# Banded attention with values stationary and transposed probabilities moving, and forget rows in the low-part matmul

## What is computed

```python
# first block, forgetting attention ("fox"): 4 heads of 64, causal
cum = jnp.cumsum(jax.nn.log_sigmoid(f_logit + f_bias), axis=1)
sc = q @ k.T * scale + cum_q - cum_k                 # then mask, softmax, @ v
# first block, chunked attention: 4 heads of 64, band of 9 chunks, bias from a table
sc = q @ k.T * scale + bias                          # then mask, softmax, @ v
# second block, banded attention ("swa"): 16 heads of 64, 2 key/value heads,
# per query block of 128: its own 128 keys and the 128 before
s = qn @ kn.T + pos_bias                             # masked to the band
m = max(max(s), sink);  p = exp(s - m)
p = p / (sum(p) + exp(sink - m))
y = ((p @ vn) * silu(z)) @ w_out
```

## Time and profile before

| | |
|---|---|
| median of 3 runs | 2418.8 us (2418.34 to 2423.13) |
| profiled execution, its own time | 2419.9 us, span 2418.1 us |
| PE busy | 2360.1 us, 98% of the span |
| DVE, ACT, POOL busy | 1507.1, 833.2, 1251.0 us |
| chain that ended last | PE 84%, DVE 6%, issue 4%, POOL 3%, ACT 2% |

### The profile page before, as it was taken

How to read it: one execution, slowest core, us unless ns; L and a number is a source line. 1 busy time by engine, 2 the same in 40 slices (tenths; PEclk the granted TensorE clock), 3 DMA queues, 4 the chain that set the end, 5 groups by cost and what they waited for, 6 DMA issues and landing times.

```text
span 2418.1 us, 32914 instructions
## 1 busy us (share of the span) xinstructions
PE 2360.1 (98%) x11836; PEld 1964.2 (81%) x11836; DVE 1507.1 (62%) x1911; ACT 833.2 (34%) x1588; POOL 1251.0 (52%) x712
## 2 busy tenths in 40 slices
PE   7999999999999999999999999999999999999998
PEld 6887788888887888888888878878888788888887
DVE  6725555624567678888877778773754866045565
ACT  4211545612433222222222433131232333055663
POOL 4533864134145666666668444563745634465523
PEclk9999999999999999999999999999999999999999
DMA  6511000031011333333331111111221113100023
GB/s 214 161 44 45 1 1 20 17 113 44 18 41 48 105 122 121 121 121 121 119 122 61 64 35 47 59 61 62 70 77 58 60 64 132 53 27 19 27 103 133
DMA packets 67270, 177.31 MB, mean 73 GB/s; under 512 B 6846, under 2 KB 13760, under 8 KB 65112
## 3 DMA queue, kind: packets, MB, share of 16 engines
q1 hardware_dynamic: 58344, 148.58, 18.6%
q10 hardware_dynamic: 8816, 27.25, 3.3%
HBM read 160.04 MB, written 15.72 MB: 73 GB/s over the span
## 4 chain that ended last, share of the span: by engine, by line
PE 84%; DVE 6%; issue 4%; POOL 3%; ACT 2%; DMA 1%; SPq 0%; DVEq 0%; POOLq 0%; ACTq 0%
PE ps L690 23%; PE ps L693 22%; PE ps L691 22%; PE ps L849 6%; PE ps L827 4%; PE ps L837 3%; POOL split_lo L1605 1%; DVE h_lo L564 1%; PE ps L705 1%; PE ps L704 1%; PE ps L703 1%; PE ps L495 1%; DVE h_lo L567 1%; DVE trail L3220 0%; ACT p L979 0%
## 5 line engine op out<-in xcount | busy, mean ns | idle before, releaser
L690 PE MATMUL ps<-h_hi,split_hi 128*128 128x512 f32 (+1 forms) x1576 | 627.2, 398 | 20.3 <-DVE h_lo L567 13.6
L691 PE MATMUL ps<-h_lo,split_hi 128*128 128x512 f32 (+1 forms) x1576 | 612.8, 389 | 0.0
L693 PE MATMUL ps<-h_hi,split_lo 128*128 128x512 f32 (+1 forms) x1576 | 547.6, 389 | 0.0
L1481 POOL TENSOR_TENSOR split_hi<-raw,cf 128x1024 fp32r<-128x1024 f32 x70 | 137.2, 1961 | 492.4 <-PE ps L693 386.9
L690 PEld LDWEIGHTS ps<-h_hi,split_hi 128*128 128x128 f32 x1576 | 297.9, 189 | 79.6 <-issue 11.4
L693 PEld LDWEIGHTS ps<-h_hi,split_lo 128*128 128x128 f32 x1576 | 297.4, 189 | 61.6
L691 PEld LDWEIGHTS ps<-h_lo,split_hi 128*128 128x128 f32 x1576 | 298.0, 189 | 55.0 <-issue 0.2
L1556 POOL TENSOR_TENSOR split_lo<-raw,split_hi 128x512 fp32r<-128x512 f32 x144 | 231.8, 1629 | 198.2 <-ACT split_hi L2493 196.6
L1605 POOL TENSOR_TENSOR split_lo<-raw,split_hi 128x512 fp32r<-128x512 f32 x84 | 127.6, 1528 | 179.8 <-ACT split_hi L2651 179.8
L1483 POOL TENSOR_TENSOR split_lo<-raw,split_hi 128x1024 fp32r<-128x1024 f32 x70 | 195.9, 2799 | 5.5
L2493 ACT CAST split_hi<-raw 128x512 fp32r<-128x512 f32 x144 | 86.8, 622 | 287.3 <-PE ps L693 214.0
(11 more groups left out here) (442 smaller groups left out, 5126.4 us busy)
## 6 DMA issues: line engine op xcount, KB each, us to landing
raw<-in_strips SPq DMA_DIRECT2D x208, 256.0 KB, 2.8
raw<-in_strips SPq DMA_DIRECT2D x86, 512.0 KB, 3.5
ada_raw<-in_ada SPq DMA_DIRECT2D x64, 512.0 KB, 3.9
memw_raw<-in_mem_strips SPq DMA_DIRECT2D x8, 512.0 KB, 6.0
xT<-in_xT ACTq DMA_DIRECT2D x4, 1024.0 KB, 8.1
x_spill_d<-xT ACTq DMA_DIRECT2D x1, 3584.0 KB, 10.0
xT<-x_spill_d ACTq DMA_DIRECT2D x2, 1792.0 KB, 9.2
out_T<-out_sb SPq DMA_DIRECT2D x14, 256.0 KB, 3.0
```

Source lines behind the costliest of these rows:

```text
L690: pe.matmul(acc[:, a:b], w_hi, hi[:, a:b], start=first, stop=False)
L691: pe.matmul(acc[:, a:b], w_hi, lo[:, a:b], start=False, stop=False)
L693: mm = pe.matmul(acc[:, a:b], w_lo, hi[:, a:b], start=False, stop=last)
L1481: pool.tensor_tensor(hi, raw[:, r, :], ones[:, 0:1].to_broadcast([P, D]), ALU.mult).then_inc(hi_split, 1)
```

## The change

Banded attention gets an order of its own, and no longer goes through `attention_plan`:

- Units run head by head (kv major in a tile). Transposed probabilities of two units (a pair, 3 or 4 blocks of 128) lie side by side in one bank; ACT copies them as the fp32r high part `swa_pt_hi` and DVE takes the low part `swa_pt_lo`.
- Values are stationary: `swa_v[kv]` holds, for each key block, 64 columns of the values' high part and 64 of the low part. For each key block the queries of one or two blocks move, once in the high and once in the low part. The outputs come out feature-major in banks 6 and 7, high-value and low-value products on different halves of the partitions; ACT copies one half (`swa_out_part`), DVE adds the other (`swa_out_sum`).
- The inverse row sums are written by DVE as 64 equal columns for each query block (`swa_inverse`, the last block in `rinv`), transposed by PE (`swa_rows`) and multiplied into `swa_z` by DVE (`swa_inverse_gate`); the outputs are multiplied in by POOL (`swa_gate`), for the last tile by DVE (`last_gate`).
- The maximum is taken as a negated minimum of -s - bias starting from the negated sink, so `floor` goes, here and in chunked attention; the exponential gets scale -1. ACT issues the exponential of unit u + 1 ahead of the copy.
- In forgetting attention the rows of cumulated logs (three fp32r parts, through `cum_d` in DRAM) and of ones lie in the free half of `fox_second` and of the low parts of the keys; the augmented matmul, `fox_aug` and the head mask go. The DMAs that bring them are issued by POOL, and PE waits for `aug_in` ahead of unit 32.
- The output product has 12 pieces inside the stage and 4 behind it; the low part of strip 2 is made by DVE.

```diff
-                dve.tensor_tensor_reduce(unit_probs(a, u), s, unit["bias"], 1.0, -3.0e38,
-                                         ALU.add, ALU.max, rowmax[:, u:u + 1]).then_inc(a["biased"], 1)
-            def floor(u):
-                unit = units[u]
-                if unit["bias"] is not None:
-                    a["n_biased"] += 1
-                    reached(dve, a, "biased", a["n_biased"])
-                    dve.tensor_scalar(negmax[:, u:u + 1], rowmax[:, u:u + 1], -3.0e38 if unit["sink"] is None else unit["sink"],
-                                      -1.0, ALU.max, ALU.mult).then_inc(a["max_ready"], 1)
+                dve.tensor_tensor_reduce(unit_probs(a, u), s, unit["bias"], -1.0, 3.0e38,
+                                         ALU.add, ALU.min, negmax[:, u:u + 1]).then_inc(a["max_ready"], 1)
...
-                       (fox_stack(h, t), fox_klo(h)[:, lo:hi], lo, hi),
-                       (fox_aug[:, h, q_tok], aug_k[:, lo:hi], lo, hi)] for lo, hi in key_banks(n)]
+                       (fox_second[:, h, q_tok], fox_klo(h)[:, lo:hi], lo, hi)] for lo, hi in key_banks(n)]
...
-            sp.wait_ge(cum_parts, 3)
-            sp.wait_ge(aug_in, 32)
-            part = [mraw[0:HEADS, 5, :].bitcast(BF16)[:, 0:T], mraw[0:HEADS, 5, :].bitcast(BF16)[:, T:2 * T],
-                    mraw[0:HEADS, 4, :].bitcast(BF16)[:, 0:T]]
-            for r in range(3):
-                sp.dma_start(aug_q[r:P:32, :], part[r]).then_inc(aug_done, 16)
-                sp.dma_start(aug_k[r + 3:P:32, :], part[r]).then_inc(aug_done, 16)
+            sp.wait_ge(cum_parts, AUG_ROWS)
+            for r, part in enumerate((mraw[0:HEADS, 5, :], mraw[0:HEADS, 4, :], cum_last[0:HEADS, :])):
+                sp.dma_start(cum_d[r], part).then_inc(cum_out, 16)
...
-            pool.wait_ge(aug_done, 16 * 6)
+            for a, b in ((0, AUG_ROWS), (2 * AUG_ROWS, HD)):
+                pool.dma_start(fox_second[HD + a:HD + b, :, :], dram["aug"][0, a:b].bitcast(F32R)).then_inc(aug_in, 16)
+            pool.wait_ge(cum_out, 16 * AUG_ROWS)
+            pool.dma_start(fox_second[HD + AUG_ROWS:HD + 2 * AUG_ROWS, :, :], cum_d.bitcast(F32R)).then_inc(aug_in, 16)
...
+                high(fox_second[0:HD, h, :], fox_q[r, h // 2, :], r)
                 high(fox_khi(h)[r, :], fox_k[r, h // 2, :], r)
                 high(fox_khi(h)[other, :], fox_k[r, h // 2, :], r)
-                low(fox_klo(h)[other, :], fox_k[r, h // 2, :], fox_khi(h)[r, :])
-                low(fox_klo(h)[r, :], fox_k[r, h // 2, :], fox_khi(h)[r, :])
-            for h in range(HEADS):
-                half_split(pool.tensor_tensor(fox_aug[:, h, :], aug_q[:, :],
-                                              cf[:, C_HEAD + h:C_HEAD + h + 1].to_broadcast([P, T]), ALU.mult))
+                low(fox_klo(h)[0:HD, :], fox_k[r, h // 2, :], fox_khi(h)[r, :])
+            for low_pair, a in ((fox_raw, 0), (fox_kr, 2)):
+                pool.dma_start(low_pair[HD:HD + AUG_ROWS, :, :], cum_d[:, a:a + 2, :].bitcast(F32R)).then_inc(aug_in, 16)
+                pool.dma_start(low_pair[HD + AUG_ROWS:P, :, :], dram["aug"][1, AUG_ROWS:HD, 0:2].bitcast(F32R)).then_inc(aug_in, 16)
...
+        SWA_AHEAD = 2
+        SWA_STEPS = range(-SWA_AHEAD, SWA_UNITS + 4)
...
+        PAIR_KEYS = ((0,), (2, 1), (4, 3), (6, 5, 7))
+        KEY_ORDER = [kb for keys in PAIR_KEYS for kb in keys]
...
+        OUT_PIECES = {OUT_FROM: (0, 0), OUT_FROM + 4: (0, 1), OUT_FROM + 5: (1, 0), OUT_FROM + 7: (0, 2), OUT_FROM + 9: (1, 1),
+                      OUT_FROM + 11: (0, 3), OUT_FROM + 13: (0, 4), OUT_FROM + 15: (1, 2), OUT_FROM + 17: (0, 5),
+                      OUT_FROM + 19: (0, 6), OUT_FROM + 21: (1, 3), OUT_FROM + 23: (1, 4)}
...
+            def swa_turn(u):
+                m, probs = u // 2, swa_probs(u)
+                n = swa_unit(u)[3] // P
+                at = 0 if u % 2 == 0 else swa_blocks(m)[1] - 2
+                if u % 2 == 0:
+                    reached(pe, att_swa, "copied_dve", m - 1)
+                    if u - 1 in ROWS_AT and rows_in_pair(ROWS_AT[u - 1][0]):
+                        tile, half = ROWS_AT[u - 1]
+                        reached(pe, att_swa, "o_gate", 2 * tile + half + 1)
+                reached(pe, att_swa, "exp_done", u + 1)
+                for j in range(n):
+                    mm = pe.transpose(swa_turned(m)[:, (at + j) * P:(at + j + 1) * P], probs[:, j * P:(j + 1) * P], ident)
+                mm.then_inc(att_swa["turned"], 1)
+            def swa_weigh(m):
+                h = m // 4
+                reached(pe, att_swa, "copied_dve", m + 1)
+                for kb in PAIR_KEYS[m % 4]:
+                    value = swa_v[h % 2][:, kb, :]
+                    for half, col0, block, n in key_spans(kb):
+                        fresh = kb % 4 == 0
+                        last = kb == NK - 1 or half == 0 and kb == 3
+                        if fresh:
+                            reached(pe, att_swa, "normed", 2 * h - 1 + half)
+                        o, blocks = bank(6 + half, n * P, col0), slice(block * P, (block + n) * P)
+                        pe.matmul(o, value, swa_pt_hi[:, blocks], start=fresh, stop=False)
+                        mm = pe.matmul(o, value, swa_pt_lo[:, blocks], start=False, stop=last)
+                    mm.then_inc(att_swa["weighted"], 1)
+            def swa_rows(tile, half):
+                reached(pe, att_swa, "inverse", sums_needed(tile, half))
+                if rows_in_pair(tile):
+                    reached(pe, att_swa, "copied_dve", (ROWS_STEP[tile, half] - 1) // 2)
+                else:
+                    pe.wait_ge(bin_q, 2 * (tile + 2) + 1)
+                    reached(pe, att_swa, "o_gate", 2 * tile + half)
+                for j in range(4):
+                    mm = pe.transpose(inverse_rows(tile, half)[:, j * P:(j + 1) * P], inverse_columns(4 * half + j), ident)
+                mm.then_inc(att_swa["o_turned"], 1)
...
+            for u in SWA_STEPS:
+                if 0 <= u < SWA_UNITS:
+                    swa_turn(u)
+                if u + SWA_AHEAD < SWA_UNITS:
+                    swa_score(u + SWA_AHEAD)
+                if u in ROWS_AT:
+                    swa_rows(*ROWS_AT[u])
+                swa_beside(u)
+                if u % 2 == 0 and 2 <= u <= SWA_UNITS:
+                    swa_weigh(u // 2 - 1)
+            early_out(0, 7)
+            for k in range(5, NK):
+                early_out(1, k)
+            reached(pe, att_swa, "o_gate", 2 * NK)
...
+            def swa_high(m):
+                h = m // 4
+                reached(act, att_swa, "turned", 2 * m + 2)
+                if h:
+                    reached(act, att_swa, "weighted", QT * (h - 1) + blocks_weighed(m))
+                act.copy(swa_pt(swa_pt_hi, m), swa_turned(m)).then_inc(att_swa["copied_act"], 1)
...
+            def swa_maximum(u):
+                reached(dve, att_swa, "scored", u + 1)
+                reached(dve, att_swa, "turned", u - 3)
+                h, n = u // QT, swa_unit(u)[3]
+                dve.tensor_tensor_reduce(swa_probs(u), swa_scores(u), swa_bias[:, h, 2 * P - n:2 * P], -1.0, neg_sinks[:, h:h + 1],
+                                         ALU.add, ALU.min, negmax[:, u:u + 1]).then_inc(att_swa["max_ready"], 1)
+            def swa_low(m):
+                reached(dve, att_swa, "copied_act", m + 1)
+                dve.tensor_tensor(swa_pt(swa_pt_lo, m), swa_turned(m), rows(swa_pt(swa_pt_hi, m)), ALU.subtract)\
+                   .then_inc(att_swa["copied_dve"], 1)
+            def swa_out_sum(h, half):
+                main, _ = head_rows(h)
+                at = swa_out(h, half)[main, :]
+                reached(dve, att_swa, "o_hi", 2 * h + half + 1)
+                dve.tensor_tensor(at, bank(6 + half)[main, :], at, ALU.add).then_inc(att_swa["normed"], 1)
+            def swa_inverse_gate(tile, half):
+                dve.wait_ge(bin_z, tile + 1)
+                reached(dve, att_swa, "o_turned", 2 * tile + half + 1)
+                at = swa_z_half(tile, half)
+                dve.tensor_tensor(at, inverse_rows(tile, half), at, ALU.mult).then_inc(att_swa["o_gate"], 1)
+            def last_gate(half):
+                tile = NK - 1
+                reached(dve, att_swa, "o_mid", 2 * tile + half)
+                reached(dve, att_swa, "normed", 4 * tile + 3 + half)
+                reached(dve, att_swa, "o_gate", 2 * tile + half + 1)
+                dve.tensor_tensor(swa_z_half(tile, half), swa_out(2 * tile, half), swa_z_half(tile, half), ALU.mult)\
+                   .then_inc(att_swa["o_mid"], 1)
...
+                if u + SWA_AHEAD < SWA_UNITS:
+                    swa_maximum(u + SWA_AHEAD)
+                if u % 2 == 1 and 0 < u < SWA_UNITS:
+                    swa_low(u // 2)
+                if u in ROWS_AT and rows_in_pair(ROWS_AT[u][0]):
+                    swa_inverse_gate(*ROWS_AT[u])
+                if u in SINK_AT:
+                    n, h, u0, u1 = SINK_AT[u]
```

(30 more changed lines are left out.)

315 lines of the change are left out of this document (184 added, 131 removed).

## The result

The changed kernel takes 2436.22 us (median of 4 runs, 2435.95 to 2436.64) against 2420.91 for the kernel before on the same chip: ratio 1.0069, 95% interval 1.0058 to 1.0081. It is slower by 0.7%. The profiled execution took 2436.64 us, its span is 2434.5 us, its mean granted clock 0.993.

What follows compares the result with a forecast made beforehand. PE, busy 98% of the span, was taken as the bound. 2419.9 - 19.2 + 24.6 + 19 + 8 - 8.3 - 1 = 2443 us, or 2442 with the median's 1.1 off; range 2412 to 2462.

Steps and rivals of the forecast that it cites:

- PE's own work: Banded attention: weighing falls from 3.30 to 2.10 us a head, all PE work from 12.81 to 11.61; -19.2 us.
- The block and what waits for it: Banded head start: DVE's 4.15 us of sums and wide reciprocals makes PE wait 2.2 or 1.8 us; +24.6 us.
- the chain: Banded head start: from last score matmul through DVE's queue until PE starts the next weighing, 6.05 us.
- the cover of 3.81 us: Banded head start: PE's work until that weighing: products, one weighing, transposes and scores; 3.81 us.
- the maximum stays: Banded attention, DVE: the maximum keeps its price, 0.34 + 0.10 us with its accumulator read.
- the walk of the last tile: Last banded tile, step by step: PE waits 24 us there and behind it, against 6 before; +19 us.
- the clock's term: Banded attention: granted clock falls after five of about 18 waits, 1.6 us each; +8 us, bounds 0 and 30.
- Forgetting attention: Forgetting stage: the matmuls against augmented rows go, and added POOL DMAs fit their cover; -8.3 us.
- Chunked attention: Chunked stage: 32 floors leave the chain maximum, exponential, transpose; -1 us (0 to -2.7).
- Rival 1: Banded attention: DVE keeps ahead, PE stays the bound; 2397 us, if the block is under about 1.9 us; chance 0.15.
- Rival 2: Banded attention: waits half absorbed, clock stays up; the 24.6 halves, last tile +10; 2410 to 2424 us; chance 0.13.
- The estimate of 8.3 ns a column: DVE reciprocals by the Trainium skill's page: block 1.06 us longer, total some 17 us higher; the trace's 6.25 was preferred.

Runs made afterwards that it cites:

- the fastest kernel: Changed kernel with 8-column reciprocals, broadcast copies on DVE, both small DVE instructions replaced, and output products and DVE's last low part reordered at the drain: 2398.14 us.
- the small reciprocals with the small instructions replaced: Changed kernel with 8-column reciprocals and broadcast copies; sink argument moved to ACT's bias, row-sum addition in the maximum's reducing form: 2404.62 us.
- the two runs with zeros added: Changed kernel plus zero-adding matmuls at four waits in the last tile: 64 of 32 columns, 2437.85 us; 32 of 512 columns, 2435.4 us.
- The small reciprocals: Changed kernel with reciprocals of 8 columns in place, and two copies broadcasting them to the 448 and 64 columns: 2406.56 us.
- the kernel with the doubled block: Changed kernel with the 448-column reciprocal issued twice, output unchanged: 2513.51 us.

## Why the prediction came out as it did

**PE's own work.** Predicted -19.2 us. In the fastest kernel, whose banded instructions on PE are the changed kernel's and whose clock is 1.00 as before, PE is busy 186.9 us of the stage, where it was 204.7: -17.8. Two heads take 23.16 us where waits are nearly gone (the small reciprocals with the small instructions replaced), for the 2 x 11.61 of the prediction. The product of 12 x 0.12 and 6 x 0.11 us a head holds.

**The block and what waits for it.** The 448-column reciprocal measured 2.953 us for 2.95, the 64-column one 0.495 for 0.55, the chain 6.06 for 6.05. The waits were 1.80 us on even heads and 1.08 + 0.37 on odd ones, for 2.2 and 1.8. So two heads came to 27.15 and not 27.3, and up to the first score of the 105th unit (start of the last tile's two-step lead) the stage is 7.8 us longer (173.8 for 166.0), where my terms gave some 9 (24.6 less 13 heads at 1.20). The chain was right, the cover of 3.81 us was a few tenths too short. I did not see one price: "the maximum stays". It takes 478 ns for 424, and 349 for 291 with 128 columns. The chunked maxima, which got the same negated minimum but start from a constant, kept their 824 ns. So the 54 to 58 ns belong to the start value that is read from SBUF, at both widths.

**The last tile and the clock.** Terms of 19 and 8 us, 27 in all. Measured from the 105th unit's score to the end of the stage: 61.3 us for 43.4, +17.9; with the 4 us put back that PE itself saved in those three heads and a bit, 22. The clock fell four times, all of them in this part, and not five times among 18 waits: behind the waits of 1.8 us in the steady part it stayed at 1.00 (window 2109 to 2284 above; in the two runs with zeros added it fell once there). It was low for 20.5 us, where five falls of 3.4 make 17, so that the time at half clock was not the error. What the falls cost was mis-sized: I took 1.6 us each, which the steady part bears out, but in the last tile much of PE's work at half clock lies in time in which it would wait for DVE. By the estimate above 3.4 to 4.8 us stand where I had 8, and 17 to 18.5 where I had 19: the walk of the last tile was near, the clock's term about twice too large.

**Forgetting attention.** Predicted -8.3, measured -6.6 in four kernels alike. The matmuls went (48 fewer), but PE now waits 1.5 us for exponentials there (L843 on ACT), where it waited 0.4: with scores done sooner, ACT's exponential is the next in line, a wait that I had not asked for. The other 0.6 us are not accounted for. The forget rows were never late: POOL's seven more DMAs found their cover.

**Chunked attention.** Predicted -1. From the first chunked score to the first banded one, with all that lies between, it is 1715.0 us for 1715.2. The floors had been hidden; DVE idle on PE's scores there had said so.

**The start.** 2.8 us that I did not forecast and that isn't the change's: 1.2 up to the wait at 232 us, and 1.6 by the missing fall of the clock behind it. The earlier trace rows showed such a fall in one execution; the same wait has it in some executions and not in others. I took it as something that follows from the wait.

**The rivals.** Rival 1 (2397 us, DVE keeps ahead) named its own condition, a block below about 1.9 us. The small reciprocals make one of some 1.7 us (0.16, 0.20, 0.43, 0.18 and an output sum of 0.69), and the time is 2406 and, with DVE's waits for POOL and the drain cleared, 2398. Rival 2 (waits half absorbed) did not hold: the steady waits kept four fifths of their forecast (1.63 us a head on average for 2.05), and the last tile cost 17 to 18.5 us and not 10; only the clock's falls were half absorbed. The estimate of 8.3 ns a column stays refuted: 2953 ns for 448 columns and 203 for 8 are 6.25 ns a column.

**The sum, as measured:** 2419.9 - 2.8 - 6.6 - 0.2 + 25.7 + 0.6 behind the stage and around the span = 2436.6 us for the profiled execution. The banded stage's 25.7 stand against 32.4 (-19.2 + 24.6 + 19 + 8). Against the forecast's 2443 for this execution, most of the difference is the clock's share (about 4 us) and the start (2.8), with forgetting attention (1.7) and chunked attention (0.8) the other way: part of the nearness of the total is errors that cancel.

## What to carry to other kernels

Broadcast after a reciprocal and not before it: here a reciprocal costs 6.25 ns for every column that it writes, a copy under 1 (425 ns for 448). An engine that is idle on average can still set the pace if its new work stands in one piece at the head of a queue; count from the last instruction that feeds it to the first that waits for what is queued behind, and compare with what the other engine has to do until then. When a burst is cut up or moved, look at what POOL does at the new place: small DVE instructions between SBUF operands may wait there until POOL's instruction ends (up to 2.16 us in these runs), and the profile books this as their busy time.

## What the runs showed of the hardware

- DVE instructions with all operands in SBUF (a tensor by a scalar, two tensors, a copy, and the reducing form too) that start during a POOL instruction last until it ends: 8 columns took up to 2.16 us, 4 columns up to 1.78. Reciprocals, and forms with one operand in PSUM, keep their durations.
- A start value read from SBUF makes the add-and-minimum form 54 to 58 ns longer, at 128 and at 256 columns.
- A fall of the granted clock costs 1.6 us where PE is the bound (28.73 for 27.16 us; 95.95, 94.3 and 92.7 us with two, one and none). In the same place and behind the same wait it comes in one execution and not in another: behind 2.08 us at 231 us in the kernel with the doubled block and not in the changed one, which are the same up to there; at the head of the last tile in one of the two runs that differ only in the drain, 1.2 us.
- 64 matmuls of 32 columns in PE's idle time did not keep the clock up; 32 of 512 columns kept it up for two thirds of the time that it had been low.
